# The last projection split by its inner dimension and spread through a blockwise triangular inversion, whose products become whole 128-row blocks

## The reference, cut to what matters

```python
# gated_delta_rule_chunked: 4 heads, 8 chunks of 64 tokens, dk = dv = 128
a_mat = lower + eye(64)                       # unit lower triangular, one per head and chunk
sol = triangular_solve(a_mat, [v_beta, k_beta * exp(g)])
u, w = sol[..., :dv], sol[..., dv:]
def step(state, inp):                         # 8 chunks in sequence
    v_new = u_c - w_c @ state
    o = (q_c * exp(g_c)) @ state + a_c @ v_new
    state = state * exp(g_last) + k_dec.T @ v_new
# hybrid_mixer
o_a = rms_norm(o_a) * silu(z_a)               # 512 wide, from the recurrence
o_b = rms_norm(diff_attention) * silu(z_b)    # 512 wide, ready long before o_a
x + concatenate([o_a, o_b]) @ w_out           # 1024 x 1024, the last projection
```

## Time and profile before

| | before |
|---|---|
| median of 3 executions | 1766.99 us (1759.88 to 1767.2) |
| profiled execution, its own time | 1769.01 us |
| its span | 1766.9 us |
| PE busy | 1703.7 us, 96% of the span, 11765 products |
| mean granted clock of TensorE | 0.968 of full |
| VectorE, ScalarE, GpSimd busy | 50%, 36%, 8% |
| DMA | 129.84 MB, 73 GB/s mean |

### The profile page before, as it was taken

The page is one execution under the profiler, slowest core; times in us unless marked ns, Lnnn a source line. Parts: engine busy times, 40 slices in busy tenths (PEclk is TensorE's granted clock), DMA queues, the critical chain, the costliest instruction groups (busy, mean ns, idle before and its releaser), DMA issues.

```text
span 1766.9 us, 27896 instructions
## 1 busy us (share of the span) xinstructions
PE 1703.7 (96%) x11765; PEld 1480.3 (84%) x11765; DVE 885.0 (50%) x1148; ACT 630.9 (36%) x968; POOL 138.9 (8%) x114
## 2 busy tenths in 40 slices
PE   7999998999999999999999999999999999877988
PEld 7997767799999999999887888888877887566977
DVE  5533547464343434565565444444566368446362
ACT  4523444424132323321223222222335356552232
POOL 1000000050000000320022000000241000002100
PEclk9999999999999999999999999999999999887599
DMA  5230001022232322232222232323364762001001
GB/s 183 72 91 13 7 1 49 25 83 85 96 96 96 95 78 88 95 96 95 94 84 92 91 95 95 93 94 95 114 91 76 83 93 43 1 10 48 3 24 72
DMA packets 137681, 129.84 MB, mean 73 GB/s; under 512 B 17645, under 2 KB 135524, under 8 KB 137588
## 3 DMA queue, kind: packets, MB, share of 16 engines
q1 hardware_dynamic: 137386, 128.44, 26.5%
q10 hardware_dynamic: 202, 0.06, 0.0%
HBM read 126.39 MB, written 2.10 MB: 73 GB/s over the span
## 4 chain that ended last, share of the span: by engine, by line
PE 91%; DVE 3%; ACT 3%; issue 1%; SPq 1%; POOL 0%; DMA 0%; ACTq 0%; DVEq 0%; POOLq 0%
PE ps L432 73%; PE ps L861 3%; PE ps L758 1%; PE ps L741 1%; PE ps L1096 1%; PE ps L1902 1%; PE ps L2204 1%; PE ps L1161 1%; PE ps L2202 1%; PE ps L766 0%; PE ps L2224 0%; PE ps L1102 0%; PE ps L1870 0%; PE ps L774 0%; PE ps L2196 0%
## 5 line engine op out<-in xcount | busy, mean ns | idle before, releaser
L405 ACT ACTIVATE w_hi<-raw 128x1024 fp32r<-128x1024 f32 (+1 forms) x227 | 239.4, 1055 | 820.3 <-PE ps L432 816.8
L432 PE MATMUL ps<-x_hi,w_hi 128*128 128x258 f32 (+4 forms) x1640 | 451.1, 327 | 3.6 <-DVE x_lo L452 2.8
L432 PE MATMUL ps<-x_lo,w_hi 128*128 128x258 f32 (+4 forms) x1640 | 444.8, 324 | 0.0
L432 PE MATMUL ps<-x_hi,w_lo 128*128 128x258 f32 (+4 forms) x1640 | 443.9, 323 | 0.0
L413 DVE TENSOR_TENSOR w_lo<-raw,w_hi 128x1024 fp32r<-128x1024 f32 (+1 forms) x227 | 295.2, 1301 | 98.4 <-ACT w_hi L405 98.3
L432 PEld LDWEIGHTS ps<-x_hi,w_hi 128*128 128x128 f32 (+2 forms) x1640 | 273.6, 188 | 34.7 <-issue 3.8
L432 PEld LDWEIGHTS ps<-x_lo,w_hi 128*128 128x128 f32 (+2 forms) x1640 | 272.6, 188 | 28.1 <-issue 2.4
L432 PEld LDWEIGHTS ps<-x_hi,w_lo 128*128 128x128 f32 (+2 forms) x1640 | 272.4, 188 | 25.9
L432 PE MATMUL ps<-a_hi,w_hi 128*128 128x258 f32 (+1 forms) x1024 | 280.9, 325 | 5.5 <-DVE gdn_LB L2394 5.2
L432 PE MATMUL ps<-a_hi,w_lo 128*128 128x258 f32 (+1 forms) x1024 | 280.7, 325 | 0.0
L432 PE MATMUL ps<-a_lo,w_hi 128*128 128x258 f32 (+1 forms) x1024 | 280.4, 325 | 0.0
(11 more groups left out here) (414 smaller groups left out, 1750.4 us busy)
## 6 DMA issues: line engine op xcount, KB each, us to landing
raw<-in_w_mlp_up SPq DMA_DIRECT2D x32, 1024.0 KB, 5.5
raw<-in_w_mlp_down SPq DMA_DIRECT2D x32, 1024.0 KB, 5.1
raw<-in_w_in SPq DMA_DIRECT2D x16, 1024.0 KB, 9.0
raw<-in_w_in_conv SPq DMA_DIRECT2D x12, 1024.0 KB, 5.1
raw<-in_w_in_attn SPq DMA_DIRECT2D x8, 1024.0 KB, 5.2
raw<-in_w_out_attn SPq DMA_DIRECT2D x4, 1024.0 KB, 5.3
raw<-in_w_out_conv SPq DMA_DIRECT2D x4, 1024.0 KB, 5.3
raw<-in_w_out SPq DMA_DIRECT2D x4, 1024.0 KB, 5.3
```

What stands on the lines that cost most here:

```text
L405: act.activation(dst, panel_view(p)[:, :, o:o + w], ACT.Copy).then_inc(w_hi_ok, 1)
L432: ins = pe.matmul(pair_of_banks[t % 2][0:m, b, 0:c], w[:, k, :], x[:, k, x0:x0 + c], start=(k == order[0] and n == 0), stop=(k == order[-1 ...
```

## The change

The last projection is divided by its inner dimension. Its four panels are now 512 rows by 512 columns (2 KB lines), first the two of rows 512 to 1023 (which meet o_b, rows 4 to 7 of `a_hi`), then the two of rows 0 to 511 (which meet o_a). A weight tile holds 4 row blocks by 256 columns, as large as before. From each come two half tiles of 128 columns: 4 row blocks by 3 terms, 12 products. There are 16 half tiles q, and each is added onto `h` by itself, so there are 16 additions in place of 8. The products are in number and size those of before, 192.

Half tiles 0 to 5 are issued in 12 pieces of 6 products between the levels' products: after each pair's D and DT in levels 1 to 4, and after y in levels 2 to 5. Half tiles 6 and 7 follow the second and the fourth sum of squares, and 8 to 15 the output's rounding, at the old place. Their splits move with them: tile 0 is split before level 1, tile 1 in it, 2 and 3 in levels 3 and 4, tile 4 between the levels and the recurrence.

The levels' products are issued by `by_heads`, head after head, on whole blocks of 128 rows and columns: 4 products a head where there were 8. y has 128 columns, D and DT take 64 (32 of each chunk). D moves to banks 4 and 5, where the pairs share a bank and so D of heads 2 and 3 waits for `tnew` of heads 0 and 1; banks 6 and 7 belong to the half tiles. The panels are asked for once `l2_normed` is at 8, earlier than by `row_pe`.

The diff, cut to what the prediction speaks of:

```diff
         T_OUT2 = len(tiles)
-        matrix_panels(W["w_out_2"][0], 0, range(0, D, PANEL))
+        HALF_PANEL = len(panels)
+        for row0 in (D // 2, 0):
+            for c in (0, D // 2):
+                panel([(W["w_out_2"][0], row0, c, PANEL)], [P, P])
...
+        def load_half_panel(sp, p):
+
+            free = panels[p - 1]["first"]
+            sp.wait_ge(w_hi_ok, free)
+            sp.wait_ge(w_lo_ok, free)
+            w, r, c, _ = panels[p]["pieces"][0]
+            src = w[r:r + D // 2, c:c + D // 2].rearrange("(k q) n -> q k n", q=P)
+            sp.dma_start(half_panel(p), src).then_inc(w_landed[p % 2], 16)
...
+        def raw_tile(t):
+            p, o, w = tiles[t]
+            return panel_view(p)[:, :, o:o + w] if p < HALF_PANEL else half_panel(p)[:, :, 2 * o:2 * o + 2 * P]
+
+        def split_tile(x, t):
+            p, _, w = tiles[t]
+            if p < HALF_PANEL:
+                return x[:, t % 2, :].rearrange("q (k n) -> q k n", k=KC)[:, :, 0:w]
+            return x[:, t % 2, :].rearrange("q (k n) -> q k n", k=KC // 2)
...
+        D_bank = lambda h: ps[:, 4 + h % 2, :]
+        D_col = lambda h: CH // 2 * (h // 2)
...
+        def half_tile_banks(q):
+
+            return ps[:, 6 + q % 2, :] if q < KC else ps[:, 2 * ((T_OUT2 + q // 2) % 2) + q % 2, :]
+
+        def half_tile_pe(pe, q, part=None):
+
+            t, x = T_OUT2 + q // 2, q % 2
+            whi, wlo = weights(t)
+            rows = (4, 5, 6, 7) if q < KC else OUT_ORDER
+            if part in (None, 0):
+                pe.wait_ge(w_lo_ok, t + 1)
+                if q >= 2 and q not in (8, 9, 10, 11):
+                    if x == 0:
+                        gd.wait(pe, "half_in", q // 2)
+                    else:
+                        pe.wait_ge(evicted, t)
+            todo = rows if part is None else rows[2 * part:2 * part + 2]
+            for k in todo:
+                if q == KC:
+                    gd.wait(pe, "o_lo", OUT_ORDER.index(k) + 1)
+                for n, (w, a) in enumerate(((whi, a_hi), (whi, a_lo), (wlo, a_hi))):
+                    ins = pe.matmul(half_tile_banks(q), w[:, k % 4, P * x:P * x + P], a[:, k, 0:SEQ],
+                                    start=(k == rows[0] and n == 0), stop=(k == rows[3] and n == 2))
+            if part in (None, 1):
+                if x == 0:
+                    ins.then_inc(gd.s["half_pe"], 1)
+                else:
+                    ins.then_inc(mm_done, 1)
...
+        def half_tile_dve(dve, q):
+
+            t, x, c = T_OUT2 + q // 2, q % 2, q % KC
+            dst = h[:, c, META:]
+            if x == 0:
+                gd.wait(dve, "half_pe", q // 2 + 1)
+            else:
+                dve.wait_ge(mm_done, t + 1)
+            ins = dve.tensor_tensor(dst, dst, half_tile_banks(q), ALU.add)
+            if x == 0:
+                ins.then_inc(gd.s["half_in"], 1)
+            else:
+                ins.then_inc(evicted, 1)
...
+        def by_heads(pair, product, done):
+
+            for h in pair:
+                for j in range(4):
+                    ins = product(h, j)
+                ins.then_inc(gd.s[done], 1)
...
+            dz.wait(pe, "out_lo", 4)
+            pieces = [0]
+            def piece():
+                half_tile_pe(pe, pieces[0] // 2, pieces[0] % 2)
+                pieces[0] += 1
             for i in range(1, 6):
+                b = LEVELS[i]
+                for pair in PAIRS if i > 1 else ():
+                    for h in pair:
+                        level_ready(i, h)
+                        gd.wait(pe, "tnew", (i - 2) * GH + h + 1)
+                        gd.wait(pe, "ttnew", (i - 2) * GH + h + 1)
+                    by_heads(pair, lambda h, j: pe.matmul(pblk(A_bank(h), j), blk(LB, h, j), blk(TM, h, j), start=True, stop=True), "y_pe")
                 if i > 1:
-                    for pair in PAIRS:
-                        for h in pair:
-                            level_ready(i, h)
-                            gd.wait(pe, "tnew", (i - 2) * GH + h + 1)
-                            gd.wait(pe, "ttnew", (i - 2) * GH + h + 1)
-                        by_chunks(pair, lambda h, r, c: pe.matmul(A_bank(h)[r, c], LB[r, h, c], TM[r, h, c], start=True, stop=True), "y_pe")
-                b = LEVELS[i]
+                    piece()
                 for pair in PAIRS:
                     for h in pair:
                         gd.wait(pe, "y", (i - 1) * GH + h + 1)
                     if i < 5:
-                        by_chunks(pair, lambda h, r, c: pe.matmul(B_bank(h)[r, c.start:c.start + CH // 2], TT[r, h, c], half(YY[r, h, c], b, 0),
-                                                                  start=True, stop=True), "d_pe")
-                    by_chunks(pair, lambda h, r, c: pe.matmul(A_bank(h)[r, c.start:c.start + CH // 2], YY[r, h, c], half(TT[r, h, c], b, 1),
-                                                              start=True, stop=True), "dt_new_pe")
+                        if pair[0]:
+                            gd.wait(pe, "tnew", (i - 1) * GH + 2)
+                        by_heads(pair, lambda h, j: pe.matmul(halves_blk(D_bank(h), j, D_col(h)), blk(TT, h, j), half(blk(YY, h, j), b, 0),
+                                                           start=True, stop=True), "d_pe")
+                    by_heads(pair, lambda h, j: pe.matmul(halves_blk(A_bank(h), j), blk(YY, h, j), half(blk(TT, h, j), b, 1),
+                                                       start=True, stop=True), "dt_new_pe")
+                    if i < 5:
+                        piece()
+            gd.wait(pe, "half_in", 3)
+            pe.wait_ge(evicted, T_OUT2 + 3)
             for h in range(GH):
                 gd.wait(pe, "ttnew", 4 * GH + h + 1)
...
+                if n >= 2:
+                    gd.wait(pe, "o_inv", n - 1)
+                pe.matmul(D_bank(n), tab["ones"][:, :], LB[:, h, :], start=True, stop=True).then_inc(gd.s["o_sum"], 1)
+                if n % 2:
+                    half_tile_pe(pe, 6 + n // 2)
...
+            split_hi(act, T_OUT2)
+            split_hi(act, T_OUT2 + 1)
             for i in range(1, 6):
+                if i in (3, 4):
+                    split_hi(act, T_OUT2 + i - 1)
                 for h in range(GH):
...
-            split_hi(act, T_OUT2)
-            split_hi(act, T_OUT2 + 1)
+            split_hi(act, T_OUT2 + 4)
...
+            split_lo(dve, T_OUT2)
             for i in range(1, 6):
+                if 2 <= i:
+                    half_tile_dve(dve, (0, 2, 3, 5)[i - 2])
                 for h in range(GH):
                     u = (i - 1) * GH + h
+                    if h == 2 and i in (2, 4):
+                        half_tile_dve(dve, i - 1 if i == 2 else 4)
+                    if h == 2 and i in (1, 3, 4):
+                        split_lo(dve, T_OUT2 + (1, 0, 2, 3)[i - 1])
                     if i == 1:
                         gd.wait(dve, "t", h + 1)
                     if i < 5:
                         gd.wait(dve, "d_pe", u + 1)
                         even = halves_in(TM[:, h, :], LEVELS[i], 0)
-                        dve.tensor_tensor(even, even, halves_of(B_bank(h), LEVELS[i]), ALU.subtract).then_inc(gd.s["tnew"], 1)
+                        dve.tensor_tensor(even, even, halves_of(D_bank(h), LEVELS[i], D_col(h)), ALU.subtract).then_inc(gd.s["tnew"], 1)
                     gd.wait(dve, "dt_new_pe", u + 1)
                     odd = halves_in(TT[:, h, :], LEVELS[i], 1)
                     dve.tensor_tensor(odd, odd, halves_of(A_bank(h), LEVELS[i]), ALU.subtract).then_inc(gd.s["ttnew"], 1)
                     if i < 5 and h >= GH // 2:
                         mask(i + 1, h)
+            split_lo(dve, T_OUT2 + 4)
...
-            split_lo(dve, T_OUT2)
-            split_lo(dve, T_OUT2 + 1)
...
+                if n == 1:
+                    half_tile_dve(dve, 6)
             split(GH - 1)
+            half_tile_dve(dve, 7)
...
+            for q in range(KC, 2 * KC):
+                if q in (8, 9, 10, 11):
+                    head = 2 * ((T_OUT2 + q // 2) % 2) + q % 2
+                    gd.wait(pe, "o_scaled", OUT_ORDER.index(head) + 1)
+                half_tile_pe(pe, q)
...
+            split_lo(dve, T_OUT2 + 5)
+            for q in range(KC, 2 * KC):
+                half_tile_dve(dve, q)
+                if q % 2 and T_OUT2 + q // 2 + 2 < T_END:
+                    split_lo(dve, T_OUT2 + q // 2 + 2)
...
-            gd.wait(sp, "row_pe", 2 * GH)
-            for p in range(tiles[T_OUT2][0], len(panels)):
-                load_panel(sp, p)
+            sp.wait_ge(gr["last"], 1)
+            dz.wait(sp, "l2_normed", 8)
+            for p in range(HALF_PANEL, len(panels)):
+                load_half_panel(sp, p)
```

(51 more changed lines are left out.)

22 lines of the change are left out of this document (9 added, 13 removed).

## The result

The changed kernel takes 1782.42 us (median of 6 executions, 1781.33 to 1785.09), the kernel before 1767.10 (6 executions, 1759.88 to 1771.3): ratio 1.0085, 95% interval 1.0064 to 1.0106, so **0.85% slower**. The forecast was 1763.8 us in a range of 1756 to 1777. The profiled execution took 1782.05 us, its span is 1780.1, 13.2 us more than before.

What follows compares the result with a forecast made beforehand. TensorE was taken as the bound, with the levels at half clock. Terms 16.9 - 1.8 + 3.1 + 1.4 - 22.8 = -3.2 us on 1769.0 gave 1765.8; the median standing 2.0 lower, 1763.8 us, range 1756 to 1777.

Steps and rivals of the forecast that it cites:

- levels: Levels' whole-block products plus twelve half-tile pieces at full clock, no added waits: 62.9 us after 45.98, +16.9 us.
- products after the levels: Eight products of four heads behind the levels, at full clock 7.1 us instead of 8.87: -1.8 us.
- stall: Start of the recurrence: tile 4's split stands ahead of VectorE's copies of u, so TensorE resumes late, +3.1 us.
- clock after the stall: Start of the recurrence: TensorE's clock may fall while it stands still, +1.4 us, bounds 0 and 2.6.
- the end, at full clock: From first sum of squares to the end: half tiles fill idle time, 32.0 us instead of 54.7, -22.8 us.
- start of the levels: Ahead of the levels: loads are asked for earlier and nothing waited for them before; no term in the sum.
- what would show it: Signs: clock near 1.00 from 1625, levels of 14.8 us, D and DT 0.89 us per head, 3 us stall.
- (1): Clock stays at half in the levels: some 1825 us, or 1795 with D and DT alone at half; chance 0.07.
- (2): Each hand-over between float32 and fp32r products costs, and D and DT run at 0.13 us: 1772 us; chance 0.16.
- (3): Start of the recurrence not held up, ScalarE's split fits between its copies: -7.7 us, 1759 us; chance 0.12.
- (4): VectorE or ScalarE ends the levels, a wait of 2 to 3 us in each of five: +10, 1776 us; chance 0.05.

Runs made afterwards that it cites:

- a1: The changed kernel with VectorE's split of tile 4 moved behind the recurrence: 1761.73 us, ratio 0.9963 to the kernel before.
- b2: The kernel before with the levels' products in whole blocks, no half tiles between them, last projection as before: 1765.68 us, one execution.
- d1: a1 with VectorE, ahead of the recurrence, waiting for ScalarE's eighth copy and then making one unread addition: 1777.38 us, one execution.
- d0: a1 with VectorE, ahead of the recurrence, only waiting for ScalarE's eighth copy, no addition: 1760.88 us, one execution.
- c1: a1 with y, D and DT packed as 64x64 products again, between the same half tiles: 1746.18 us, ratio 0.9855 to the kernel before.
- c4: The program of c1 measured again, side by side with c3: 1745.06 us, ratio 0.9874 to the kernel before.
- c2: a1 with y left in whole blocks and only D and DT packed: 1742.04 us, one execution.
- c3: The program of c2 measured again in rounds: 1750.00 us, ratio 0.9897 to the kernel before.

## Why the prediction was wrong

Its steps against the two profiled executions:

| step | predicted | measured |
|---|---|---|
| levels | +16.9 | 63.04 - 45.98 = +17.1 |
| products after the levels | -1.8 | 7.21 - 8.87 = -1.7 |
| stall | +3.1 | +3.0 |
| clock after the stall | +1.4 | 14.75 in the recurrence, 2.85 after it: **+17.6** |
| the end, at full clock | -22.8 | 32.29 (a1, 1718.80 to 1751.09) - 54.71 = -22.4 |
| start of the levels | 0 | -0.35 |
| sum | -3.2 | +13.2 |

**The step that failed** is "While it stands still, its clock may fall", priced at half of a stretch of 2.63 us, with bounds of 0 and 2.6 us. That the clock may fall was right. The price was taken from a place where 512-column products of the last projection followed the idle stretch; what follows here is the recurrence, whose products never raised the clock in 38.21 us. (Half of 2.63 is 1.3, not 1.4; that changes nothing.) I had even used the recurrence's 1.00 as evidence that such products earn the full clock. The row shows only that they keep it: before, they began after 8.87 us of whole blocks, without a wait. The levels before, TensorE 93% busy at 0.51, were the second warning, and the nearer one: there TensorE stood still for 2.35 us at 1630.03 and its small products then ran at half for 37 us (the windows at b2). The prediction read the levels as small products "without pause" and their waits as "under a microsecond per level"; that holds for levels 3 to 5 (some 0.9 us each), not for the one ahead of level 2. The true upper bound was the price paid there: everything up to the next dense products at half, which is the recurrence (233 records) and the sums.

The Trainium skill, page "TensorE: Matmul & The Clock Gate", Part 1, says that the lower level is the default and that activity of the engine releases it. The end of the program agrees: in half tile 6 the clock came back. The recurrence does not, with TensorE busy in all of its 38.21 us at 0.50; here the measurement decides.

Point by point of "what would show it": the clock was 1.00 from 1625 to the stall; the level 14.9 us for 14.8, no waits on `tnew`; D and DT 1.73 and 1.79 us a pair, 0.87 and 0.89 a head; the stall 3.0 us, ending on VectorE's copy. Half tile 8 starts 9.1 us after the first sum where the clock is full (a1), with 0.47 us of waiting for `a_lo` against 0.9 charged; in the changed kernel it starts 11.9 us after.

The rivals: (1) half clock in the levels did not occur, nor in b2 without the half tiles. The grounds for expecting it full were in part wrong (the recurrence had been entered at full clock), so that this term came out right by more than its reasons. (2) A piece between float32 blocks took 1.39 to 1.45 us for 1.38, so a hand-over costs a few hundredths, not 0.1; 16 records of D took 1.73 us, 0.11 each, not 0.13. (3) The stall came; where a1 takes it away, the time is 1761.7, near the 1759 of this rival. (4) VectorE worked 25.9 of the 63.04 us and ended nothing. The rival that happened was none of the four. It is the forecast with its smallest term off by 16 us; every other term came within 0.4 us.

## What to carry to other kernels

A wait of TensorE can have two prices: its own length, and a clock at half until the next products that can raise it. Here 0.93 us cost only itself, 1.53 us and more cost the clock too. Before costing a new stall, look at what follows it, and take the second price from there rather than from another stall. Where small products must follow a wait, let some dense work stand directly ahead of them; and before a form of product is given up as slow, look at which clock it was measured, and for a wait just ahead of the place where that clock fell.

## What was not expected of the hardware

- The recurrence holds either level: 23.47 us at 1.00 and 38.21 at 0.50 with the same products in the same order, but the full one was lost where 1.5 us or more of idleness stood directly ahead.
- 1.5 us of idleness ahead of it instead of 0.9 cost 16.5 us (d1 against d0, one execution each); in d1 the clock fell after the resumption, not in the gap.
- The packed levels stay at 0.50 once they have lost the clock behind a wait of 2.35 us (before), and at 1.00 with a piece of six 512-column products after every two groups and no such wait (c1, c4). Whether packed products without pieces and without the wait would keep a full clock for good, or only for some time, as in level 1, no run here tells.
- The attention stretch ahead, 1500 to 1600, got 0.90 in one execution of c2's program and 0.85 in the others. With it went levels that began 7 to 9 us earlier, more than the whole difference between c3 and c4. Single executions of this kernel cannot tell smaller differences apart.
